# Last RMSNorm and residual of a two-layer encoder on token-major tiles, with the residual input transposed first

## The chip, the cores and the metric

The kernel runs on one core of a Trainium2 chip. The metric is the device time of one execution in microseconds (us). Before the change three runs gave a median of 3404.63 us (3402.58 to 3406.06).

## The reference

The kernel computes a two-layer streaming encoder step, in float32, for 1024 prompt tokens and 8 x 16 tokens of running streams. Only the very last operation matters here: the residual update that ends layer 1.

```
def _rmsnorm(x, g):
    x32 = x.astype(jnp.float32)
    y = x32 * lax.rsqrt(jnp.mean(x32 * x32, axis=-1, keepdims=True) + EPS) * g.astype(jnp.float32)
    return y.astype(x.dtype)

for layer in range(DEPTH):
    ...                                   # mLSTM (layer 0) or differential attention (layer 1)
    x = x + _rmsnorm(h, norm_g[layer, 1])
    h = _swiglu(_rmsnorm(x, norm_g[layer, 2]), ffn_w_in[layer], ffn_w_out[layer])
    x = x + _rmsnorm(h, norm_g[layer, 3])
return x, ...                             # y_prompt (1, 1024, 1024) and y_sample (8, 16, 1024)
```

## The kernel before

Prompt and sample tokens are processed together as 1152 tokens. The stream lies transposed in SBUF: F0 is `[128, 8, 1152]`, with the feature within a block of 128 on the partitions, the 8 blocks (k) next, and the tokens on the free axis. F1 has the same layout and holds what a layer adds, here the output h of the last FFN. The 1152 tokens are cut into 9 tiles of 128 (`tile(i)`) for transposes and stores, and into 3 chunks of 384 (`TC`) for matmuls.

The order of the work is written out by hand, one program for each engine, with semaphores between them. There is no scheduler. PSUM has 8 banks of 512 floats per partition. Matmul outputs of 1152 tokens use two triples of banks in turn, 0 to 2 for even groups and 3 to 5 for odd ones (`G(o)`); `group_free` says that a triple was evacuated. The last group of the last FFN ("ffn1") adds its 8 blocks of output into F1 one by one: TensorE fills a triple (lines 1615, 1619 and 1621 are the three products of a split float32 matmul), VectorE adds it to F1 (L2085), ScalarE squares the finished block (L1818) into one of two buffers SQX, and VectorE adds the squares into ACCX (L2015, L2017).

After the last block ("post3") the kernel before does this:

- TensorE multiplies ACCX and the last square by a matrix of ones (L1711, L1714), so that the sum of squares of each token stands on all 128 partitions.
- ScalarE takes a logarithm (L1824) and an exponential (L1827) of it, each with a load of its function table, which gives 1/rms in RS, `[128, 1152]`.
- VectorE, chunk by chunk (`last_residual`), multiplies the 8 blocks of F1 by gain and RS (L2055) and adds blocks 0 to 3 into F0 (L2059); GpSimd adds blocks 4 to 7 (L1596).
- Chunk by chunk TensorE transposes the finished F0 (`store_y_pe`, L1423, 8 transposes of 128x128 for each tile of 128 tokens, into pairs of banks), ScalarE copies each tile from PSUM into one of three buffers XL (L1432), and SyncE stores it (L1438). XL is used again once its store has landed (`y_sent`).

Of the kernel before, what the change touches and what calls it, by code (L numbers as in the profile page):

```python
# [18 lines left out]
ALU = mybir.AluOpType  # L19
# [3 lines left out]
P = 128  # L23
D = 1024
# [5 lines left out]
NT = T // P  # L30
# [108 lines left out]
def build(nc, x_prompt, x_sample, state_C, state_n, state_m, cache_k, cache_v, norm_g, mlstm_w_in,  # L139
# [4 lines left out]
    with ctx, nc.allow_non_contiguous_dma(reason="a few gates, stabilisers and tables of rows"):  # L144
        def sem(name):
            return ctx.enter_context(nc.semaphore(name))
# [50 lines left out]
        r = Region(XB, XB + 2 * FB)  # L197
        ACCX = r("ACCX", [P, T])
        SQX = [r(f"SQX{i}", [P, T]) for i in range(2)]

        r = Region(*W)
        XL = [r(f"XL{i}", [P, D]) for i in range(3)]
# [182 lines left out]
        def tile(i):  # L385
            return slice(i * P, (i + 1) * P)
# [1021 lines left out]


        y_tr = sem("y_tr")  # L1410
        y_cp = sem("y_cp")
        y_sent = [sem(f"y_sent{i}") for i in range(3)]

        def store_y_pe(pe):
            for i in range(NT):
                if i % 3 == 0:

                    pe.wait_ge(res_ready[0], 3 * KT // 2 + i // 3 + 1)
                    pe.wait_ge(res_ready[1], 3 * KT // 2 + i // 3 + 1)
                if i >= 4:  # L1420
                    pe.wait_ge(y_cp, i - 3)
                for k in range(KT):
                    mm = pe.transpose(PS[:, 2 * (i % 4) + k // 4, (k % 4) * P:(k % 4 + 1) * P], F0[:, k, tile(i)], ident)  # L1423
                mm.then_inc(y_tr, 1)

        def store_y_act(act):
            for i in range(NT):
                act.wait_ge(y_tr, i + 1)
                if i >= 3:
                    act.wait_ge(y_sent[i % 3], 16 * (i // 3))  # L1430
                b = 2 * (i % 4)
                act.activation(XL[i % 3][:, :], PS[:, b:b + 2, :].rearrange("p b c -> p (b c)"), ACT.Copy).then_inc(y_cp, 1)  # L1432
            act.wait_ge(nsv_sent, VSTORED)

        def store_y_sp(sp):
            for i in range(NT):
# [87 lines left out]
        @blocks.gpsimd  # L1524
        def _(pool):
            pool.memset(WRAW[0][:, :, :], 0.0)
            pool.memset(BG[:, :], 0.0).then_inc(s_zero, 1)
            pool.memset(EPSC[:, :], EPS).then_inc(w_split, 2)
            pool.memset(HALF[:, :], -0.5).then_inc(unit_free, 1)
            pool.memset(ZERO[:, 0:1], 0.0).then_inc(group_free[0], 1)  # L1530
            pool.memset(ZERO[:, 1:2], 0.0).then_inc(group_free[1], 1)
            pool.memset(ZERO[:, 2:3], 0.0).then_inc(hf_ready, 1)
            pool.memset(ZERO[:, 3:4], 0.0).then_inc(nsv_sent, 16)
            pool.memset(ZERO[:, 4:5], 0.0).then_inc(nt_cp, 1)

            def split(par, u, landed):
                pool.wait_ge(w_landed[par], landed)
                pool.wait_ge(unit_free, u + 1)

                pool.tensor_tensor(WHI[par][:, :, :], WRAW[par][:, :, :], bc(bc(ZERO[:, 0], KT), P), ALU.add)  # L1540
                pool.drain()
                pool.tensor_tensor(WLO[par][:, :, :], WRAW[par][:, :, :], WHI[par][:, :, :].bitcast(F32),  # L1542
                                   ALU.subtract).then_inc(w_split, 1)

            def pair(first, i):

                for j in range(2):
                    par = (first + j) % 2
                    split(par, first + 2 * i + j, 16 * ((first + j) // 2) + 16 + (0 if par else 16) + 16 * i)

            def single(u):
                split(u % 2, u, 16 * (u // 2) + 16 + (0 if u % 2 else 16))

            def residual(n):

                for k in range(1, KT, 2):
                    pool.wait_ge(res_mul, n * KT // 2 + k // 2 + 1)
                    pool.tensor_tensor(F0[:, k, :], F0[:, k, :], F1[:, k, :], ALU.add).then_inc(res_ready[1], 1)
                pool.drain()

            def run(first, n):
                with pool.Fori(0, n // 2) as i:
                    pair(first, i)

            pool.drain()
            split(0, 0, 32)
            run(U0["q_m"], 24)
            single(U0["out_m"])
            mlstm_pool(pool)
            single(U0["out_m"] + 1)  # L1570
            run(U0["out_m"] + 2, 6)
            single(U0["ffn0"])
            residual(0)
            single(U0["ffn0"] + 1)
            pool.wait_ge(f1_dead, 1)
            pool.memset(F1[:, :, :], 0.0).then_inc(f1_zero, 1)
            run(U0["ffn0"] + 2, 64)
            single(U0["q_a"])
            residual(1)
            single(U0["q_a"] + 1)  # L1580
            run(U0["q_a"] + 2, 22)
            single(U0["out_a"])
            attention_pool(pool)
            single(U0["out_a"] + 1)
            run(U0["out_a"] + 2, 6)
            single(U0["ffn1"])
            residual(2)
            single(U0["ffn1"] + 1)
            pool.wait_ge(f1_dead, 2)
            pool.memset(F1[:, :, :], 0.0).then_inc(f1_zero, 1)  # L1590
            run(U0["ffn1"] + 2, 64)

            for c in range(NC):
                cols = slice(c * TC, (c + 1) * TC)
                pool.wait_ge(res_mul, 3 * KT // 2 + c + 1)
                pool.tensor_tensor(F0[:, 4:8, cols], F0[:, 4:8, cols], F1[:, 4:8, cols], ALU.add).then_inc(res_ready[1], 1)  # L1596


        @blocks.tensor
        def _(pe):  # L1600
# [103 lines left out]
            def norm_sum(name, acc=None, sq=None):  # L1704

                o, n = G0[name], NORMS.index(name)
                free_wait(o, 0, 0)
                if acc is not None:
                    pe.wait_ge(acc_ready, POSTS.index(name) + 1)
                    for c in range(NC):  # L1710
                        pe.matmul(G(o)[:, c, :], ones, acc[:, chunk(c)], start=True, stop=False)  # L1711
                    pe.wait_ge(sq_ready, squares_ready(name, KT - 1))
                    for c in range(NC):
                        mm = pe.matmul(G(o)[:, c, :], ones, sq[:, chunk(c)], start=False, stop=True)  # L1714
                else:
                    for k in range(KT):
                        pe.wait_ge(sq_ready, squares_ready(name, k))
                        for c in range(NC):
                            mm = pe.matmul(G(o)[:, c, :], ones, SQ[k % 2][:, chunk(c)], start=k == 0, stop=k == KT - 1)
                            if k == 0 and c == 0:  # L1720
                                mm.then_inc(unit_free, 1)
                        if k < KT - 1:
                            mm.then_inc(sq_used, 1)
                mm.then_inc(group_ready, 1)
# [78 lines left out]
            norm_sum("post2", ACC, SQ[1])  # L1803
            norm_sum("pre2")
            ffn("ffn1", 6)
            norm_sum("post3", ACCX, SQX[1])
            store_y_pe(pe)


        @blocks.scalar  # L1810
        def _(act):
            def squares(name, src, ready=None, sq=SQ):
                for k in range(KT):
                    if ready is not None:
                        ready(k)
                    if squares_used(name, k - 2) > 0:
                        act.wait_ge(sq_used, squares_used(name, k - 2))
                    act.activation(sq[k % 2][:, :], src[:, k, :], ACT.Square).then_inc(sq_ready, 1)  # L1818

            def root(name):  # L1820

# [176 lines left out]
            root("pre2")  # L1998
            high_norm("ffn1", 4 * KT)
            ffn("ffn1")  # L2000
            squares("post3", F1, lambda k: act.wait_ge(group_free[(G0["post3"] - KT + k) % 2], (G0["post3"] - KT + k) // 2 + 2), SQX)
            root("post3")
            store_y_act(act)


        @blocks.vector
        def _(dve):
# [13 lines left out]
            def rstd(name):  # L2021
                dve.wait_ge(rs_ready, NORMS.index(name) + 1)
# [15 lines left out]
            def residual(gain):  # L2038

                dve.drain()  # L2040
                for k in range(KT):
# [3 lines left out]
                        dve.tensor_tensor(F0[:, k - 1, :], F0[:, k - 1, :], F1[:, k - 1, :], ALU.add).then_inc(res_ready[0], 1)  # L2045
                    else:
                        dve.drain()

            def last_residual(gain):

                dve.drain()
                for c in range(NC):
                    cols = slice(c * TC, (c + 1) * TC)
                    for k in (4, 5, 6, 7, 0, 1, 2, 3):
                        w = dve.scalar_tensor_tensor(F1[:, k, cols], F1[:, k, cols], gain(k), RS[:, cols], ALU.mult, ALU.mult)  # L2055
                        if k == 7:
                            w.then_inc(res_mul, 1)
                    dve.drain()
                    dve.tensor_tensor(F0[:, 0:4, cols], F0[:, 0:4, cols], F1[:, 0:4, cols], ALU.add).then_inc(res_ready[0], 1)  # L2059

            def ffn(name):
                o0, l = G0[name], FFN_L[name]
# [119 lines left out]
            updated(dve, 2, KT - 1)  # L2182
            norm_split(6, lambda k: GN[:, 1, 2, k:k + 1])
            ffn("ffn1")
            rstd("post3")
            last_residual(lambda k: GN[:, 1, 3, k:k + 1])


# [26 lines left out]
```

## Time and profile before

| | |
|---|---|
| median of three runs | 3404.63 us |
| the profiled execution's own time | 3402.93 us |
| its span (first to last instruction of the trace) | 3401.1 us |
| last matmul of the FFN begins to end | about 3351.6 us into the span |
| from there to the end of the span | about 49.5 us |

All figures of the trace are of that one profiled execution. Busy time is not at once time on the critical path: the chain of waits says what the end waited for, and the timeline of one engine says when each instruction began. In the timeline neighbours of the same kind are merged ("x24"), and the time of a merged row runs from the first start to the last end. PE is TensorE, PEld its loads of the stationary operand, DVE VectorE, ACT ScalarE, POOL GpSimd. PEclk is the granted TensorE clock: 1.00 is 2.4 GHz and 0.50 is 1.2 GHz, and a value between them is a stretch with both.

### The profile page before, as it was taken

How to read it: one execution, taken by the hardware profiler on the slowest of the kernel's cores; microseconds unless marked ns; L12 is line 12 of the kernel's file. 1: busy time of each engine (PE TensorE's matmuls, PEld its weight loads, DVE VectorE, ACT ScalarE, POOL GpSimd, SP SyncE). 2: the span in 40 equal slices, each digit the busy share in tenths (PEclk: the TensorE clock that was granted, in tenths of full speed). 3: DMA queues.
4: the chain of work that ended last, by engine and by line, in shares of the span. 5: the costliest groups of instructions: out<-in, count | busy, mean ns of one | idle time of the engine just before them, and what ended most of it. 6: DMA issues, size and time to landing. Idle time of an engine off the chain costs nothing.

```text
span 3401.1 us, 45274 instructions
## 1 busy us (share of the span) xinstructions
PE 3120.9 (92%) x18309; PEld 2947.2 (87%) x18309; DVE 1122.6 (33%) x1561; ACT 727.2 (21%) x1205; POOL 1003.4 (30%) x523
## 2 busy tenths in 40 slices
PE   6999987979999999997889977888979999999996
PEld 6999876959999999996889945566959999999995
DVE  4100254252222222225220058865152222222226
ACT  4111242240000000002222157644140000000002
POOL 2333100433333333333323322110443333333331
PEclk8999877989999999999999989998989999999998
DMA  4121301201111111110212220046201111111111
GB/s 152 43 77 55 94 32 56 93 19 44 44 43 37 43 43 43 40 40 25 87 44 86 88 83 26 13 151 216 94 18 44 44 43 40 40 43 43 43 37 56
DMA packets 237697, 200.90 MB, mean 59 GB/s; under 512 B 8545, under 2 KB 202494, under 8 KB 237074
## 3 DMA queue, kind: packets, MB, share of 16 engines
q1 hardware_dynamic: 194402, 147.93, 14.0%
q10 hardware_dynamic: 43184, 51.46, 4.5%
q8 instruction: 74, 1.21, 0.2%
q14 instruction: 37, 0.30, 0.0%
HBM read 166.30 MB, written 33.06 MB: 59 GB/s over the span
## 4 chain that ended last, share of the span: by engine, by line
PE 80%; DVE 6%; issue 6%; ACT 2%; DVEq 2%; POOL 1%; POOLq 1%; ACTq 1%; DMA 1%; SPq 0%
PE PS L1615 23%; PE PS L1619 23%; PE PS L1621 23%; PE PS L1042 1%; DVE F L2042 1%; PE PS L1088 1%; PE PS L1122 1%; PE PS L1072 1%; PE PS L513 1%; PE PS L1678 1%; PE PS L490 1%; DVE PS L1307 1%; DVE F L2055 1%; DVE XLO L2026 1%; DVEq L1308 1%
## 5 line engine op out<-in xcount | busy, mean ns | idle before, releaser
L1540 POOL TENSOR_TENSOR WHI<-WRAW,ZERO 128x1024 fp32r<-128x1024 f32 x197 | 373.6, 1897 | 1805.6 <-PE PS L1615 1774.3
L1615 PE MATMUL PS<-XHI,WHI 128*128 128x384 f32 x3672 | 848.2, 339 | 63.3 <-DVE XLO L2026 62.9
L1619 PE MATMUL PS<-XLO,WHI 128*128 128x384 f32 x3672 | 839.6, 336 | 0.0
L1621 PE MATMUL PS<-XHI,WLO 128*128 128x384 f32 x3672 | 838.6, 336 | 0.0
L1615 PEld LDWEIGHTS PS<-XHI,WHI 128*128 128x128 f32 x3672 | 656.6, 190 | 74.1 <-issue 55.8
L1619 PEld LDWEIGHTS PS<-XLO,WHI 128*128 128x128 f32 x3672 | 660.7, 189 | 0.0
L1621 PEld LDWEIGHTS PS<-XHI,WLO 128*128 128x128 f32 x3672 | 659.3, 189 | 0.0
L1542 POOL TENSOR_TENSOR WLO<-WRAW,WHI 128x1024 fp32r<-128x1024 f32 x197 | 487.6, 2475 | 28.1
L2085 DVE TENSOR_TENSOR F<-F,PS 128x1152 f32<-128x1152 f32 x176 | 238.3, 1354 | 460.3 <-PE PS L1621 460.3
L2070 DVE TENSOR_TENSOR HF<-PS,SG 128x1152 f32<-128x1152 f32 x44 | 59.7, 1358 | 668.3 <-PE PS L1621 668.3
L1900 ACT ACTIVATE HHI<-HF 128x1152 fp32r<-128x1152 f32 x44 | 51.4, 1168 | 1060.6 <-DVEq L2071 1060.6
L1615 PE MATMUL PS<-HHI,WHI 128*128 128x384 f32 x1056 | 243.5, 338 | 5.3 <-DVE HLO L2073 5.3
L1619 PE MATMUL PS<-HLO,WHI 128*128 128x384 f32 x1056 | 242.8, 338 | 0.0
L1621 PE MATMUL PS<-HHI,WLO 128*128 128x384 f32 x1056 | 242.7, 338 | 0.0
L1615 PEld LDWEIGHTS PS<-HHI,WHI 128*128 128x128 f32 x1056 | 189.6, 188 | 6.6 <-DVE HLO L2073 5.9
L1621 PEld LDWEIGHTS PS<-HHI,WLO 128*128 128x128 f32 x1056 | 190.1, 188 | 0.0
L1619 PEld LDWEIGHTS PS<-HLO,WHI 128*128 128x128 f32 x1056 | 189.9, 188 | 0.0
L2073 DVE TENSOR_TENSOR HLO<-HF,HHI 128x1152 fp32r<-128x1152 f32 x44 | 139.1, 3161 | 56.4 <-ACT HHI L1900 56.4
L1895 ACT ACTIVATE SG<-PS 128x1152 f32<-128x1152 f32 x44 | 50.0, 1136 | 421.3 <-PE PS L1621 421.3
L1307 DVE CUSTOM_DVE_ANT_0 PS<-PS,BROW 128x128 f32<-128x128 f32 (+7 forms) x128 | 97.7, 763 | 21.1 <-issue 17.6
L2032 DVE SCALAR_TENSOR_TENSOR XN<-F,GALL,RS 128x1152 f32<-128x1152 f32 x40 | 58.7, 1467 | 128.3 <-PE PS L1621 86.3
L1042 PE MATMUL PS<-F,F 64*128 64x512 f32 (+3 forms) x384 | 84.1, 545 | 18.2 <-ACTq L1203 14.5
(278 smaller groups left out, 2480.4 us busy)
## 6 DMA issues: line engine op xcount, KB each, us to landing
WRAW<-in_ffn_w_in_dram SPq DMA_DIRECT2D x88, 512.0 KB, 3.7
WRAW<-in_ffn_w_out_dram SPq DMA_DIRECT2D x44, 512.0 KB, 3.6
KC<-in_cache_k_dram SPq DMA_DIRECT2D x16, 1024.0 KB, 9.2
VC<-in_cache_v_dram SPq DMA_DIRECT2D x16, 1024.0 KB, 6.2
WRAW<-in_mlstm_w_in_dram SPq DMA_DIRECT2D x24, 512.0 KB, 3.8
xs_scratch<-F ACTq DMA_DIRECT2D x2, 4608.0 KB, 13.3
F<-xs_scratch ACTq DMA_DIRECT2D x2, 4608.0 KB, 14.4
WRAW<-in_kv_w_dram SPq DMA_DIRECT2D x16, 512.0 KB, 3.8
```

The lines of the kernel that those rows point to most:

```text
L1042: mm = pe.matmul(sflat(n, j, w)[:, c:e], F1[64 * j:64 * j + 64, h, tile(i)], F0[64 * j:64 * j + 64, h, c:e], start=True, stop=True)
L1307: dve.tensor_tensor_reduce(s, s, BROW[n % 2][:, SEQ - w:], -1.0, 3e38, ALU.add, ALU.min, stat(n, 4 + j))
L1540: pool.tensor_tensor(WHI[par][:, :, :], WRAW[par][:, :, :], bc(bc(ZERO[:, 0], KT), P), ALU.add)
L1542: pool.tensor_tensor(WLO[par][:, :, :], WRAW[par][:, :, :], WHI[par][:, :, :].bitcast(F32), ALU.subtract).then_inc(w_split, 1)
L1615: mm = pe.matmul(out[:, c, :], wh, rhs_hi[:, chunk(c)], start=first, stop=False)
L1619: pe.matmul(out[:, c, :], wh, rhs_lo[:, chunk(c)], start=False, stop=False)
L1621: mm = pe.matmul(out[:, c, :], wl, rhs_hi[:, chunk(c)], start=False, stop=last)
L1900: act.activation(HHI[:, t, :].rearrange("p (c t) -> p c t", c=NC), HF[:, :, :], ACT.Copy).then_inc(hh_ready, 1)
L2032: dve.scalar_tensor_tensor(XN[k % 2][:, :], F0[:, k, :], gain(k), RS[:, :], ALU.mult, ALU.mult).then_inc(xn_ready, 1)
L2070: dve.tensor_tensor(HF[:, :, :], G(o), SG[:, :, :], ALU.mult).then_inc(group_free[o % 2], 1)
L2073: dve.tensor_tensor(HLO[:, t, :].rearrange("p (c t) -> p c t", c=NC), HF[:, :, :], HHI[:, t, :].rearrange("p (c t) -> p c t", c=NC).bitcas ...
L2085: dve.tensor_tensor(f, f, G(o), ALU.add).then_inc(group_free[o % 2], 1)
```

## The change

The last norm is applied to token-major tiles, after the transposes. Both operands are now transposed: tile by tile F0 (the residual, kind "x") and F1 (the FFN's output, kind "r"), 18 turns of 8 transposes in place of 9.

- Each turn writes one of three pairs of PSUM banks in rotation: (6, 7), (0, 1), (3, 4). The order is x0, x1, x2, r0, x3, r1, x4, r2, x5, r3, x6, r4, x7, r5, x8, r6, r7, r8. Turn n waits for the evacuation of turn n-3.
- The first three turns of x stand ahead of the sum of squares on TensorE. The sum of squares is formed with ACCX and the last square as the stationary operand and one column of ones moving, so that it comes out as one number for each token and partition (bank 2, 9 columns).
- VectorE turns these 9 columns into mean + eps, GpSimd raises them to the power -0.5 (RT, `[128, 9]`).
- ScalarE multiplies each finished block of F1 by its gain, in place, behind its square. It no longer computes logarithm and exponential.
- x0 to x2 are copied from PSUM into XT by VectorE, x3 to x8 by ScalarE. XT lies where the low half of the split FFN input (XLO) was.
- VectorE joins scaling and residual in one instruction for each tile: XL = r (in PSUM) * RT + XT. `last_residual` and GpSimd's additions are gone.

The core of the diff (waits that only mirror these dependencies are kept where a step uses them):

```
+        XT = at("XT", XB + FB, [P, NT, D])
...
+        Y_E = 3 * (G0["post3"] % 2)
+        Y_L = 3 - Y_E
+        Y_BANKS = (6, Y_E, Y_L)
+        Y_ORDER = [("x", i) for i in range(3)]
+        for i in range(NT):
+            Y_ORDER += [("r", i)] + ([("x", i + 3)] if i + 3 < NT else [])
...
         def store_y_pe(pe):
+            def turn(n):
+                kind, i = Y_ORDER[n]
+                if n >= 3:
+                    prev, m = Y_ORDER[n - 3]
+                    if prev == "r":
+                        pe.wait_ge(y_cp, m + 1)
+                    elif m < 3:
+                        pe.wait_ge(y_xd, m + 1)
+                    else:
+                        pe.wait_ge(y_xa, m - 2)
+                src = F0 if kind == "x" else F1
+                dst = y_pair(kind, i)
+                for k in range(KT):
+                    mm = pe.transpose(dst[:, k * P:(k + 1) * P], src[:, k, tile(i)], ident)
+                mm.then_inc(y_tr, 1)
+
+            turn(0)
+            pe.wait_ge(group_free[G0["post3"] % 2], G0["post3"] // 2 + 1)
+            turn(1)
+            pe.wait_ge(group_free[(G0["post3"] + 1) % 2], (G0["post3"] + 1) // 2 + 1)
+            turn(2)
+            pe.wait_ge(acc_ready, POSTS.index("post3") + 1)
+            pe.wait_ge(sq_ready, squares_ready("post3", KT - 1))
+            for t in range(NT):
+                pe.matmul(PS[:, Y_E + 2, t:t + 1], ACCX[:, tile(t)], ones[:, 0:1], start=True, stop=False)
+                mm = pe.matmul(PS[:, Y_E + 2, t:t + 1], SQX[1][:, tile(t)], ones[:, 0:1], start=False, stop=True)
+            mm.then_inc(y_sum, 1)
+            pe.wait_ge(y_gain, KT)
+            for n in range(3, len(Y_ORDER)):
+                turn(n)
...
+        def store_y_act(act):
+            for i in range(3, NT):
+                act.wait_ge(y_tr, y_turned("x", i))
+                act.activation(XT[:, i, :], y_pair("x", i), ACT.Copy).then_inc(y_xa, 1)
...
+        def store_y_dve(dve):
+            for i in range(3):
+                dve.wait_ge(y_tr, y_turned("x", i))
+                dve.tensor_copy(XT[:, i, :], y_pair("x", i)).then_inc(y_xd, 1)
+            dve.wait_ge(y_sum, 1)
+            dve.tensor_scalar(RT[:, :], PS[:, Y_E + 2, 0:NT], 1.0 / D, EPS, ALU.mult, ALU.add).then_inc(y_mean, 1)
+            dve.wait_ge(y_rstd, 1)
             for i in range(NT):
+                dve.wait_ge(y_tr, y_turned("r", i))
                 if i >= 3:
+                    dve.wait_ge(y_xa, i - 2)
+                    dve.wait_ge(y_sent[i % 3], 16 * (i // 3))
+                else:
+                    dve.drain()
+                dve.scalar_tensor_tensor(XL[i % 3][:, :], y_pair("r", i), RT[:, i:i + 1], XT[:, i, :], ALU.mult, ALU.add
+                                         ).then_inc(y_cp, 1)
+
+        def store_y_pool(pool):
+            pool.wait_ge(y_mean, 1)
+            pool.tensor_tensor(RT[:, :], RT[:, :], bc(HALF[:, 0], NT), ALU.pow).then_inc(y_rstd, 1)
...
                     act.activation(sq[k % 2][:, :], src[:, k, :], ACT.Square).then_inc(sq_ready, 1)
+                    if gain is not None:
+                        act.activation(src[:, k, :], src[:, k, :], ACT.Copy, scale=gain(k)).then_inc(y_gain, 1)
...
-            norm_sum("post3", ACCX, SQX[1])
...
-            root("post3")
...
-            rstd("post3")
-            last_residual(lambda k: GN[:, 1, 3, k:k + 1])
+            store_y_dve(dve)
```

On TensorE, at the end of the program before (CST is the identity or the ones, F0 the stream, waits in brackets):

```order
L1621 MATMUL PS<-HHI,WLO_57 128x384 x3
L1711 MATMUL PS<-ACCX,CST 128x384 [waits acc_ready,group_free0]
L1711 MATMUL PS<-ACCX,CST 128x384 x2
L1714 MATMUL PS<-SQX_75,CST 128x384 [waits sq_ready]
L1714 MATMUL PS<-SQX_75,CST 128x384 x2
L1423 MATMUL PS<-CST,F_49 128x128 [waits res_odd,res_even]
L1423 MATMUL PS<-CST,F_49 128x128 x23
```

The same place in the changed program (F_49 is F0, F_50 is F1; L1450 is the transpose, L1461 and L1462 the sums, which stand nine times):

```order
L1678 MATMUL PS<-HHI,WLO_57 128x384 x3
L1450 MATMUL PS<-CST,F_49 128x128 x24
L1461 MATMUL PS<-CST,ACCX 128x1
L1462 MATMUL PS<-CST,SQX_75 128x1
...
L1450 MATMUL PS<-CST,F_50 128x128 x8
L1450 MATMUL PS<-CST,F_49 128x128 x8
...
L1450 MATMUL PS<-CST,F_50 128x128 x24
```

24 transposes of F0 now stand between the last matmul of the FFN and the sums, and no transpose waits for a residual any more.

On VectorE, from the last addition of squares to the end, before:

```order
L2017 TENSOR_TENSOR ACCX<-ACCX,SQX_74 128x1152 [waits sq_ready]
L2055 SCALAR_TENSOR_TENSOR F_50<-F_50,GALL,RS 128x384 [waits rs_ready]
L2055 SCALAR_TENSOR_TENSOR F_50<-F_50,GALL,RS 128x384 x7
L2059 TENSOR_TENSOR F_49<-F_49,F_50 128x4x384
L2055 SCALAR_TENSOR_TENSOR F_50<-F_50,GALL,RS 128x384 x8
```

and in the changed program (the last row stands for tiles 3 to 8, with the three XL buffers in turn):

```order
L2075 TENSOR_TENSOR ACCX<-ACCX,SQX_74 128x1152 [waits sq_ready]
L1477 COPY XT<-PS 128x1024 [waits y_tr] x3
L1479 TENSOR_SCALAR RT<-PS 128x9 [waits y_sum]
L1488 SCALAR_TENSOR_TENSOR XL_77<-PS,RT,XT 128x1024 [waits y_tr,y_rstd]
L1488 SCALAR_TENSOR_TENSOR XL_78<-PS,RT,XT 128x1024 [waits y_tr]
L1488 SCALAR_TENSOR_TENSOR XL_79<-PS,RT,XT 128x1024 [waits y_tr]
L1488 SCALAR_TENSOR_TENSOR XL_77<-PS,RT,XT 128x1024 [waits y_sent0,y_xa,y_tr]
```

VectorE's 24 multiplications and 3 additions gave way to 3 copies, one small instruction and 9 joined instructions that read PSUM and wait for a turn, for a copy of x and for a store.

## Rows read from the trace of the kernel before

**Rows 1.** The page, chain that ended last: shares of the span by engine.

```profile
PE 80%; DVE 6%; issue 6%; ACT 2%; DVEq 2%; POOL 1%; POOLq 1%; ACTq 1%; DMA 1%; SPq 0%
```

**Rows 2.** Chain in order of time, window 3350 to 3402: start us, us, what.

```profile
3351.05 0.55 PE PS L1621 x3
...
3353.07 1.36 DVE ACCX L2017
...
3354.62 3.85 PE PS L1711 x6
3358.47 1.95 PE PS L1714 x6
...
3360.44 1.22 ACT RS L1824
...
3364.28 0.62 DVE F L2055
...
3390.34 1.77 DVE F L2059
...
3392.15 3.61 PE PS L1423 x16
```

**Rows 3.** Timeline of ScalarE at the end: start us, us, line, shapes, idle before.

```profile
3353.01 1.16 ACT L1818 ACTIVATE SQX<-F 128x1152 f32<-128x1152 f32 x1 [2.01 <-DVE F L2085]
...
3395.79 1.94 ACT L1432 ACTIVATE XL<-PS 128x1024 f32<-128x1024 f32 x2 [0.61 <-PE PS L1423]
```

**Rows 4.** TensorE in stretches of 1 us: busy (instructions), granted clock, DMA share, GB/s.

```profile
3353.00:3354.00 1.00, 0.00 (x0) 1.00 0.00 0
...
3355.00:3356.00 1.00, 1.00 (x2) 0.50 0.00 0
...
3358.00:3359.00 1.00, 1.00 (x5) 1.00 0.00 0
...
3394.00:3395.00 1.00, 1.00 (x7) 0.50 0.00 0
...
3396.00:3397.00 1.00, 0.63 (x6) 1.00 1.02 422
```

**Rows 5.** Timeline of TensorE: transposes at 1.2 and 2.4 GHz, 128-column float32 passes.

```profile
18.80 1.09 PE L1773 MATMUL PS<-CST,XL 128*128 128x128 f32 x8 [1.98 <-DMA XL<-in_x_prompt_dram]
...
2245.03 1.95 PE L1088 MATMUL PS<-VP,PTS 128*128 128x128 f32 x16
...
2271.11 1.97 PE L1122 MATMUL PS<-CST,KC 128*128 128x128 f32 x16
...
3373.65 5.17 PE L1423 MATMUL PS<-CST,F 128*128 128x128 f32 x24 [13.25 <-DVE F L2059]
```

**Rows 6.** Timeline of TensorE in the mLSTM stage: 256-column and 1-column float32 matmuls.

```profile
386.23 0.68 PE L513 MATMUL PS<-CT,F 128*128 128x256 f32 x2
386.75 0.28 PE L514 MATMUL PS<-CTN,F 128*128 128x1 f32 x2
386.89 0.68 PE L490 MATMUL PS<-VN,WT 128*128 128x256 f32 x2
```

**Rows 7.** Groups of VectorE by shape: busy us, mean ns, idle before.

```profile
L2032 DVE SCALAR_TENSOR_TENSOR XN<-F,GALL,RS 128x1152 f32<-128x1152 f32 x40 | 58.7, 1467 | 128.3 <-PE PS L1621 86.3 <-ACT RS L1827 29.4 <-ACTq L1941 9.3
...
L1364 DVE COPY KTS<-PS 128x1024 f32<-128x1024 f32 x16 | 19.6, 1225 | 14.3 <-PE PS L1122 14.1
L790 DVE SCALAR_TENSOR_TENSOR F<-PS,GALL,F 128x128 f32<-128x128 f32 x72 | 19.4, 343 | 0.9
...
L776 DVE SCALAR_TENSOR_TENSOR CT<-CT,WS,PS 128x256 f32<-128x256 f32 x32 | 13.2, 476 | 1.0
...
L755 DVE TENSOR_TENSOR DEN<-PS,DEN 128x4 f32<-128x4 f32 x9 | 1.5, 162 | 0.7
```

**Rows 8.** Groups of GpSimd by shape, the two powers.

```profile
L1002 POOL TENSOR_TENSOR RSTD<-MSQ,HALF 128x8 f32<-128x8 f32 x8 | 13.1, 1639 | 1.2
...
L440 POOL TENSOR_TENSOR DEN<-DEN,HALF 128x4 f32<-128x4 f32 x9 | 9.1, 1009 | 186.9 <-ACT DEN L636 186.9
```

**Rows 9.** DMA issues, window 3370 to 3402: count, KB each, median us to landing.

```profile
out_dram<-XL SPq DMA_DIRECT2D x9, 512.0 KB, 2.6
```

More of the change, by code:

```diff
@@ L1410, in build @@
         y_tr = sem("y_tr")
+        y_gain = sem("y_gain")
+        y_sum = sem("y_sum")
+        y_mean = sem("y_mean")
+        y_rstd = sem("y_rstd")
+        y_xd = sem("y_xd")
+        y_xa = sem("y_xa")
         y_cp = sem("y_cp")
         y_sent = [sem(f"y_sent{i}") for i in range(3)]
-        def store_y_pe(pe):
-            for i in range(NT):
[L1416 to L1424, printed above, removed]
@@ L1426, in store_y_act @@
-        def store_y_act(act):
-            for i in range(NT):
-                act.wait_ge(y_tr, i + 1)
-                if i >= 3:
[L1430 to L1433, printed above, removed]
+        Y_E = 3 * (G0["post3"] % 2)
+        Y_L = 3 - Y_E
+        Y_BANKS = (6, Y_E, Y_L)
+        Y_ORDER = [("x", i) for i in range(3)]
@@ new lines, in build, with y_turned, y_pair @@
+        for i in range(NT):
+            Y_ORDER += [("r", i)] + ([("x", i + 3)] if i + 3 < NT else [])
+        def y_turned(kind, i):
+            return Y_ORDER.index((kind, i)) + 1
+        def y_pair(kind, i):
+            b = Y_BANKS[Y_ORDER.index((kind, i)) % 3]
+            return PS[:, b:b + 2, :].rearrange("p b c -> p (b c)")
+        def store_y_pe(pe):
+            def turn(n):
[27 more added lines that the diff above has]
+                turn(n)
@@ new lines, in store_y_act @@
+        def store_y_act(act):
+            for i in range(3, NT):
+                act.wait_ge(y_tr, y_turned("x", i))
+                act.activation(XT[:, i, :], y_pair("x", i), ACT.Copy).then_inc(y_xa, 1)
+            act.wait_ge(nsv_sent, VSTORED)
+        def store_y_dve(dve):
[5 more added lines that the diff above has]
+            dve.wait_ge(y_rstd, 1)
+            for i in range(NT):
+                dve.wait_ge(y_tr, y_turned("r", i))
+                if i >= 3:
+                    dve.wait_ge(y_xa, i - 2)
[4 more added lines that the diff above has]
+                                         ).then_inc(y_cp, 1)
@@ L1591, in _ @@
             run(U0["ffn1"] + 2, 64)
[L1593 to L1596, printed above, removed]
+            store_y_pool(pool)
         @blocks.tensor
@@ L1811, in _, with squares @@
         def _(act):
-            def squares(name, src, ready=None, sq=SQ):
+            def squares(name, src, ready=None, sq=SQ, gain=None):
                 for k in range(KT):
@@ L2000, in _ @@
             ffn("ffn1")
-            squares("post3", F1, lambda k: act.wait_ge(group_free[(G0["post3"] - KT + k) % 2], (G0["post3"] - KT + k) // 2 + 2), SQX)
-            root("post3")
+            squares("post3", F1, lambda k: act.wait_ge(group_free[(G0["post3"] - KT + k) % 2], (G0["post3"] - KT + k) // 2 + 2), SQX,
+                    lambda k: GN[:, 1, 3, k:k + 1])
             store_y_act(act)
@@ L2047, in residual @@
                         dve.drain()
[L2049 to L2059, printed above, removed]
             def ffn(name):
```

## The prediction

> **What bounds the kernel now.** I read the chain of waits first, over the whole span and then over its last 50 us, after that the timelines of the engines there, and last the groups by shape for the price of each new operation. Over the whole span TensorE holds 80% of the chain [rows 1]. The change does not touch that part: it works behind the last FFN matmul. There the chain is another one [rows 2]. TensorE ends at 3351.6 us, and VectorE's last addition of squares sets the start of the column sums at 3354.62. Sums, logarithm and exponential take until 3364.28, and from there VectorE alone sets the pace: 24 multiplications and 3 additions up to 3392.11. Only then can the last three tiles be transposed. ScalarE's last copy ends at 3395.79 + 1.94 = 3397.73 [rows 3], and store and end take 3401.1 - 3397.73 = 3.37. Of the 46.5 us between 3354.62 and 3401.1 TensorE works 5.8 for the sums [rows 2] and three times about 5 for the transposes. So what is to be gained is at most what lies between a TensorE that never waits and these 46.5 us, and the question is what limits the new tail.
>
> **The change part by part.** All sums are against the profiled execution (3402.93 us with a span of 3401.1); it lies 1.7 us under the median of the runs shown, to which I apply the difference.
>
> *Turns of x0 to x2.* A turn is 8 transposes. At the granted clock of 1.00, 8 take 1.09 us and 16 take 1.97 [rows 5]: 0.88 by the difference, 0.98 by half of the longer row. I take 0.94. At 0.50, 24 take 5.17, so a turn is 1.72. After the FFN, from 3353 to 3354, the clock is still 1.00 [rows 4], so three turns take 2.8 us, from 3351.6 to 3354.4. TensorE waited in this stretch anyway, so they cost nothing. If they came cold, they would end at 3356.8 and cost 2.2. The other wait in front of x2, for the evacuation of the last FFN block, ends when the addition of squares begins (3353.07), before x2 is due.
>
> *Gains on ScalarE.* 8 more instructions of 128x1152, each like the square of 1.16 us. A square came after 2.01 us of idling [rows 3], so a block lasts 3.17 and two such instructions (2.3) fit. The last gain ends at 3353.01 + 1.16 + 1.17 = 3355.3, well before r0 is turned. Cost nothing; without this cover at most the one behind the last square, 1.2.
>
> *Sums.* 18 matmuls with one moving column. A float32 matmul stands as two passes in the trace (three of 384 columns are x6 in [rows 2], one of 1 column is x2 in [rows 6]), so 36 passes, each with its own stationary load. No stretch of only such passes exists. From above: two 256-column and two 1-column passes take 386.89 - 386.23 = 0.66 together, 0.165 each, which gives 5.9 us. From below: a 1-column pair moves the next start by 0.14, 0.07 each, 2.5 us. Nearest is a train of 128-column passes with a new stationary operand each, 16 in 1.95 [rows 5], 0.122 each: 4.4 us. Start 3354.6 as before, end 3359.0. VectorE's three copies of x (1.225 each, [rows 7]) run beside it, 3354.5 to 3358.2.
>
> *1/rms.* VectorE's small instruction 0.16 [rows 7]; the power on GpSimd took 1.009 for 4 columns and 1.639 for 8 [rows 8], 0.157 a column, so 1.80 for 9; below, 1.0 if columns cost nothing, above, 3.3 if it were twice the 8-column row. Three handovers at 0.1 (before, the handover into the sums was 0.19: 3353.07 + 1.36 to 3354.62 in [rows 2]). The result is there at 3361.25. This wait is new and exposed: TensorE has r0, x3 and r1 to turn meanwhile (2.8 us, to 3361.8), but the pair for x4 is that of r0.
>
> *Joined instructions.* Scale and add from PSUM: 343 ns for 128 and 476 for 256 elements [rows 7], 1.04 ns an element, so 1.27 us for 1024. From below 1.22 (a copy), from above 1.47 (the same kind with 1152 elements, from SBUF). r0 is done at 3362.5, and x4 starts at 3362.6.
>
> *The other 12 turns.* 12 x 0.94 = 11.3, TensorE ends at 3373.9. This holds if the ring does not stall: a turn may start when the evacuation three turns back is over, so two turns (1.88) must cover 0.2 + 1.27 + 0.1 = 1.57 of the joined instruction, and 1.02 of a copy fits more easily. Stores: a buffer comes round after three tiles, 5.6 us; joined instruction plus store is 1.27 + 3.37 = 4.6, and a store lands in 2.6 [rows 9]. At 1.47 the ring is still at 1.77.
>
> *End.* r6, r7 and r8 are turned one behind the other, faster than VectorE empties them: r6 is turned at 3372.0, three joined instructions from 3372.2 end at 3376.0. With 3.37 for store and end the span is 3379.4: 21.7 us less. The forecast is 3404.6 - 21.7 = 3383.
>
> **A page against the trace: the clock.** In the last tile group before, only transposes ran; the granted clock was 0.50 at 3394 to 3395 and 1.00 at 3396 to 3397, with TensorE busy throughout since 3392.15 [rows 2, 4]. So a dense train of transposes raised the clock here, and one that is warm should keep it. The Trainium skill, "TensorE: Matmul & The Clock Gate", section "PE-mode transpose", says the opposite: transposes do not count as activity for the clock gate, so it does not open for them. By that rule the tail would run at 1.2 GHz; the rows above contradict it.
>
> **The rivals.** A: cold throughout, as a mechanism of this kernel: the clock falls to 0.50 behind the last FFN matmul and stays there, as it did at 3355 after 3 us without work [rows 4]. x0 to x2 end at 3356.8, 36 sums at 0.215 take 7.7 (to 3364.5), 15 turns at 1.72 take 25.8 (to 3390.3), then 0.3 + 1.27 + 3.37: 3395.2, only 5.9 less than before: 3398.7. For it: every long train of transposes at the end began at 0.50 [rows 5]. Against it: these began after idling, and the clock rose within them. This is also the time by the page's rule.
>
> B: cold for a part. One-column passes leave the array nearly empty, and so may the wait for 1/rms. The clock fell after 3 us without work and was at 1.00 again from 3358 [rows 4], some 3 us later; half of that is lost, 1.5 for one such stretch and 3 for two: 3384.5 to 3386, and 3389 if it happens again among the turns. For it: nothing in the trace shows a stretch of one-column passes that kept the clock.
>
> C: the ring runs in lockstep, each turn beginning only when the one before is evacuated, because the three pairs don't overlap as the code lets them. A turn then costs 1.72 + 0.3 + 1.27 + 0.1 = 3.4 (cold, as TensorE is half idle), 15 of them from 3362.4 (sums cold, 3354.6 + 7.7) end at 3413 with their evacuation, plus 3.4: 3416.8, 15.7 slower, 3420. It decides from (3401.1 - 3.4 - 3359.0) / 15 = 2.6 us a turn. Against it: the code names the evacuation three turns back, and before, three tiles were turned in one train of 5.17 us [rows 5] while ScalarE emptied the first of them.
>
> D: the early turns are not hidden, because x0 to x2 start only with the sums' data: 2.8 later, 3385.8.
>
> **How the numbers follow.** Forecast 0.55, B 0.25, D 0.05, A 0.10, C 0.03, and 0.02 for something smaller between A and no change. The unknown prices move the forecast by -1.9 (sums at 2.5) - 0.8 (power) - 0.2 (joined) and by +1.5 (sums at 5.9) + 1.5 (power) + 0.8 (joined): 3380.1 to 3386.7. B reaches to 3389. With A partly in, and 1 us for the spread of the median, the range is 3379.5 to 3392. About 0.2% (6.8 us) is what a measurement of this kernel can tell from no change: faster needs less than 3397.8. That is all of forecast, B and D, half of the 0.02, and of A the case in which the clock comes back for some turns (0.05): 0.91. Within 0.2%: the rest, 0.06. Slower: C, 0.03.
>
> **What would show each step.** Transposes of F0 directly behind the last FFN matmul, in under 3 us, and the sums starting at about 3354.6. Sums over at about 3359 with the clock at 1.00. The power on GpSimd 1.8 us long, with TensorE idle for under 1 us before x4. After that turns of 0.94 us with VectorE not behind, and joined instructions of 1.27. The granted clock in the turns tells the forecast from A and B, the distance between turns from C, and the start of the first transposes from D. The forecast is wrong if the joined instruction takes much over 1.5, since then VectorE with 9 of them becomes the bound, or if the clock falls for longer than the ring takes.

## The result, and the profile after

The changed kernel takes 3384.82 us (median of 5 runs, 3380.29 to 3388.72) against 3405.11 before (5 runs), a ratio of 0.9941 with a 95% interval of 0.9929 to 0.9952. Timed again with five runs it took 3380.6 against 3402.65, 0.9934 (0.9921 to 0.9948). The forecast was 21.7 us less; the medians differ by 20.3 and 22.1.

A good measure inside a profile is the *tail*: from the end of VectorE's last addition of squares to the end of the span. Before, it ran from 3353.07 + 1.36 = 3354.43 [rows 2] to 3401.1: 46.7 us. After, in the profiled execution (3380.29 us, the fastest of the five; span 3378.5), the chain of waits reads as follows (start us, us, what):

```profile
3352.77 1.36 DVE ACCX L2075
...
3354.23 0.38 PE PS L1461 x2
...
3358.43 13.18 PE PS L1450 x104
...
3371.64 0.37 DVE XL L1488
```

The addition ends at 3354.13, so the tail is 24.4 us, against 25.0 in the forecast. Between this addition and the last tiles TensorE alone is on the chain. Its timeline (start us, us) shows two trains of transposes, where three trains of 24 stood before (one of them is in [rows 5]):

```profile
3351.12 2.78 PE L1450 MATMUL PS<-CST,F 128*128 128x128 f32 x24
...
3358.29 15.05 PE L1450 MATMUL PS<-CST,F 128*128 128x128 f32 x120
```

The first 24 stand where TensorE was idle before; they end at 3353.9, ahead of the sums. The other 15 turns are one unbroken row: the ring of three pairs did not stall by more than 0.1 us here. VectorE, in the place of the multiplications of [rows 2], with GpSimd's power and ScalarE's last gain:

```profile
3354.31 3.49 DVE L1477 COPY XT<-PS 128x1024 f32<-128x1024 f32 x3 [0.18 <-issue]
3358.47 0.17 DVE L1479 TENSOR_SCALAR RT<-PS 128x9 f32<-128x9 f32 x1 [0.67 <-PE PS L1462]
3360.61 1.28 DVE L1488 SCALAR_TENSOR_TENSOR XL<-PS,RT,XT 128x1024 f32<-128x1024 f32 x1 [1.97 <-POOL RT L1493]
...
3371.64 3.67 DVE L1488 SCALAR_TENSOR_TENSOR XL<-PS,RT,XT 128x1024 f32<-128x1024 f32 x3 [0.46 <-PE PS L1450]
```

```profile
3358.72 1.80 POOL L1493 TENSOR_TENSOR RT<-RT,HALF 128x9 f32<-128x9 f32 x1 [32.69 <-DVE RT L1479]
```

```profile
3353.78 1.24 ACT L1876 ACTIVATE F<-F,GALL 128x1152 f32<-128x1152 f32 x1
```

VectorE has 9 instructions of 1.28 us, with gaps before the first seven, where it had 27 without. The granted clock differs from the forecast's picture (stretches of 1 us: busy, instructions, granted clock, DMA share, GB/s; [rows 4] before):

```profile
3357.00:3358.00 1.00, 1.00 (x11) 1.00 0.00 0
3358.00:3359.00 1.00, 1.00 (x8) 0.63 0.00 0
...
3361.00:3362.00 1.00, 1.00 (x8) 0.67 0.00 0
3362.00:3363.00 1.00, 1.00 (x11) 1.00 0.30 106
```

At the end of the one-column sums it fell to 0.50, and 3.4 us later, under transposes alone, it was back. With the first transposes slowed, the wait before x4 that the forecast had put in does not appear.

### The profile page after: what moved, and what is told of

It reads as the page before. It is cut to its first block, busy times and chain, and to the rows that moved or that the text cites. A ratio compares the mean times of both kernels' runs of the same rounds, so it can differ in the third digit from the quotient of the medians.

```text
span 3378.5 us, 45448 instructions
## 1 busy us (share of the span) xinstructions
PE 3122.8 (92%) x18405; PEld 2951.6 (87%) x18405; DVE 1110.3 (33%) x1547; ACT 728.3 (22%) x1206; POOL 996.6 (29%) x521
## 3 DMA queue, kind: packets, MB, share of 16 engines
q8 instruction: 75, 1.23, 0.2%
## 4 chain that ended last, share of the span: by engine, by line
PE 81%; issue 6%; DVE 5%; ACT 2%; DVEq 2%; POOL 1%; POOLq 1%; ACTq 1%; DMA 1%; SPq 0%
PE PS L1672 23%; PE PS L1676 23%; PE PS L1678 23%; PE PS L1044 1%; DVE F L2100 1%; PE PS L1090 1%; PE PS L1124 1%; PE PS L1074 1%; PE PS L515 1%; DVE PS L1309 1%; PE PS L1735 1%; PE PS L492 1%; DVEq L1310 1%; PE PS L1135 0%; PE PS L500 0%
```

## The experiments

Where a run has no timed rounds, its verdict comes from the tail of its profile. The front of the program, which no experiment touched, turned out to end anywhere between 3351.2 and 3363.6 us.

**The changed kernel again.** No edit.

> The changed kernel once more, to see what its spread of 8 us comes from. The tail is counted from the end of VectorE's last addition of squares to the end of the span; it was 46.7 us before the change and 24.4 us in the first profile after it, with one stretch of 3 us at a granted clock of 0.50 behind the sums. Theory (the spread lies in front of the tail): tail 24 to 25 us again, and the addition of squares ends at another time of the span by several us. Rival (the clock in the tail makes the spread): another number of stretches at 0.50 in the tail, each worth about 1.5 us, so a tail of 23 or of 26 to 32 us, and the addition of squares within 1 us of 3354.1.

Measured: 3380.6 us, tail 3353.37 to 3379.3, 25.9 us. The addition of squares ended 0.8 us earlier than in the first profile, and the tail was 1.5 longer. The clock fell already within the sums and stayed down twice as long:

```profile
3356.00:3357.00 1.00, 1.00 (x11) 1.00 0.00 0
3357.00:3358.00 1.00, 1.00 (x7) 0.51 0.00 0
...
3363.00:3364.00 1.00, 1.00 (x7) 0.58 0.76 295
3364.00:3365.00 1.00, 1.00 (x11) 1.00 0.03 4
```

Neither side came out whole. The tail lies outside the theory's 24 to 25 us, and the addition ended within 1 us of 3354.1, as the rival had it. What this run shows is that a longer stretch at 0.50 made the tail 1.5 us longer. Where the rest of the 8 us comes from, two profiles cannot tell; the runs below point to the front.

**Sums with 128 columns moving.**

```
-pe.matmul(PS[:, Y_E + 2, t:t + 1], ACCX[:, tile(t)], ones[:, 0:1], start=True, stop=False)
+pe.matmul(PS[:, Y_E + 2, 8 * t:8 * t + P], ACCX[:, tile(t)], ones, start=True, stop=False)
... (the same for SQX[1]; the mean is read at every eighth column)
```

> The column sums with 128 columns of ones moving in place of one, the same 36 passes. Theory (one-column passes leave the array empty, and therefore the clock falls behind them): granted clock 1.00 from the FFN to the last turn; the sums take 4.0 to 4.4 us as before, turns r0 and x3 take 0.94 in place of 1.7, but x4 then waits for the joined instruction of r0, which ends about 1.3 us after 1/rms, so the tail is only 0.6 us shorter: 23.8. Rival 1 (transposes do not count as work for the clock, so it falls wherever the FFN is over): 0.50 behind the sums as before, tail 24.4. Rival 2 (the clock falls in the wait for 1/rms instead): 0.50 some 3 us later, tail 24 to 25.

Measured: 3381.24 us (ratio 0.9936, 0.9923 to 0.995), tail 3351.16 to 3375.6, 24.4 us. Clock and turns:

```profile
3355.00:3356.00 1.00, 1.00 (x11) 1.00 0.00 0
...
3358.00:3359.00 1.00, 0.16 (x2) 1.00 0.00 0
...
3362.00:3363.00 1.00, 1.00 (x12) 1.00 0.55 213
```

```profile
3355.38 2.78 PE L1450 MATMUL PS<-CST,F 128*128 128x128 f32 x24
3359.07 5.46 PE L1450 MATMUL PS<-CST,F 128*128 128x128 f32 x48 [0.90 <-DVE XL L1488]
3364.99 5.46 PE L1450 MATMUL PS<-CST,F 128*128 128x128 f32 x48 [0.46 <-DVE XL L1488]
```

The sums last as long as with one column (3351.26 to 3355.38, 4.1 us), and the clock stays at 1.00 to the last turn. That speaks for the theory. But the tail is no shorter: what the clock gave, TensorE lost in the wait for 1/rms before x4 (0.90, where the prediction had 0.8) and in a second wait of 0.46 that no theory had named. The 0.6 us were a miss.

**x0 to x2 turned behind the sums.**

```
-            turn(0)
             pe.wait_ge(group_free[G0["post3"] % 2], G0["post3"] // 2 + 1)
-            turn(1)
...
-            turn(2)
...
-            for n in range(3, len(Y_ORDER)):
+            for n in range(len(Y_ORDER)):
... (and VectorE forms mean + eps ahead of its copies of x)
```

> x0 to x2 turned behind the sums in place of ahead of them (and VectorE's mean ahead of its copies of x, so that 1/rms is not held up). Theory (the early turns only fill time in which TensorE waited anyway): TensorE idle for about 3 us behind the FFN, the tail longer by the three turns, 2.8 us, and by what the clock loses: as before the change it falls in the idle time, the sums then run at 0.50 for about 3 us (1.5 more) while the stretch at 0.50 behind the sums is gone or stays: tail 27 to 29. Rival (the early turns were not what counts, since 1/rms is waited for anyway): tail within 1 us of 24.4.

Measured: tail 3363.59 to 3395.3, 31.7 us, 7.3 longer than the first profile's 24.4 and more than either theory said. TensorE (timeline, and clock in stretches of 1 us):

```profile
3363.89 0.35 PE L1458 MATMUL PS<-CST,ACCX 128*128 128x1 f32 x2 [3.15 <-DVEq L2074]
...
3370.39 13.42 PE L1450 MATMUL PS<-CST,F 128*128 128x128 f32 x96
3384.71 5.46 PE L1450 MATMUL PS<-CST,F 128*128 128x128 f32 x48 [0.90 <-DVE XL L1485]
```

```profile
3364.00:3365.00 1.00, 1.00 (x10) 1.00 0.00 0
...
3366.00:3367.00 1.00, 1.00 (x7) 0.50 0.00 0
...
3374.00:3375.00 1.00, 1.00 (x7) 0.50 0.00 0
...
3376.00:3377.00 1.00, 1.00 (x11) 1.00 0.00 0
```

Behind 3.15 us of idling the clock was down from 3365.2 to 3375.4, three times as long as in the first profile of the changed kernel. The sums took 3363.89 to 3370.39, 6.5 in place of 4.1 (2.4 more, counted to the first turn behind them); three turns more stand behind them (2.8); the cold turns behind the sums cost about 1.1 more; and a wait of 0.90 came in, since VectorE waited for a store. Together 7.2. The early turns thus gave about a third of the whole gain: 2.8 us because idle time was filled, some 3.5 because the clock stayed up, and 0.9 because no store was waited for. This rests on one profile.

**The joined instruction in two steps.**

```
-dve.scalar_tensor_tensor(XL[i % 3][:, :], y_pair("r", i), RT[:, i:i + 1], XT[:, i, :], ALU.mult, ALU.add)...
+dve.tensor_scalar(XL[i % 3][:, :], y_pair("r", i), RT[:, i:i + 1], None, ALU.mult)
+dve.drain()
+dve.tensor_tensor(XL[i % 3][:, :], XL[i % 3][:, :], XT[:, i, :], ALU.add).then_inc(y_cp, 1)
```

> The joined instruction of VectorE split in two, scale from PSUM into XL and then add XT. Theory (TensorE bounds the tail only because one VectorE instruction of 1.28 us does a tile): VectorE needs 1.25 + 0.1 + 1.2 = 2.5 us a tile, more than the 1.9 of two turns, so 9 x 2.5 = 22.6 from 1/rms at 3360.6 on, tail 32 us (7.9 longer), TensorE waiting for VectorE at most turns. Rival (TensorE's 15 turns set the pace whatever VectorE does): only the last tiles show, tail 25.7 to 28.

Measured: tail 3353.63 to 3387.1, 33.5 us, 9.1 longer than the first profile of the changed kernel. The clock was down from 3357.2 to 3364.0, as long as in the second profile (25.9 us); against that one the tail is 7.6 longer, near the 7.9 of the theory. Every second turn of TensorE now waits for VectorE:

```profile
3369.11 1.97 PE L1450 MATMUL PS<-CST,F 128*128 128x128 f32 x16 [0.71 <-DVE XL L1490]
3371.60 1.97 PE L1450 MATMUL PS<-CST,F 128*128 128x128 f32 x16 [0.53 <-DVE XL L1490]
3374.10 1.97 PE L1450 MATMUL PS<-CST,F 128*128 128x128 f32 x16 [0.53 <-DVE XL L1490]
```

A period is 2.49 us a tile, VectorE's 1.28 + 1.23 with little between them. TensorE bounds the tail only because one VectorE instruction empties and finishes a tile.

**Six output buffers, with the wide sums.**

```
-        XL = [r(f"XL{i}", [P, D]) for i in range(3)]
+        XL = [r(f"XL{i}", [P, D]) for i in range(6)]
... (a joined instruction waits for a store from tile 6 on only)
```

> The wide sums and six output buffers XL in place of three, so that no joined instruction of tiles 3 to 5 waits for a store. With wide sums alone TensorE waited twice for VectorE in the turns, 0.90 us before x4 (1/rms) and 0.46 before the turn behind r3's joined instruction, whose buffer still held r0; tail 24.4 us. Theory (the second wait is the store of r0, which shares the DMA engines with that of r1): it goes, the first stays, tail 23.9. Rival (the ring of three pairs makes both waits): both stay, tail 24.4.

Measured: tail 3354.73 to 3378.5, 23.8 us. Only the wait for 1/rms is left:

```profile
3358.95 2.78 PE L1450 MATMUL PS<-CST,F 128*128 128x128 f32 x24
3362.64 10.70 PE L1450 MATMUL PS<-CST,F 128*128 128x128 f32 x96 [0.90 <-DVE XL L1489]
```

As the theory said, the second wait was an output buffer that still waited for its store: with wide sums alone the store of r0 landed 4.5 us after it was issued (the median was 2.7), and the joined instruction of r3 began 0.1 us later. The other half of the theory, that this store was late because it shared the DMA engines with that of r1, does not hold. In the first profile of the changed kernel the store of r0 took 4.5 us as well, though the next was issued only 2.3 us behind it and the engines moved almost nothing between 3364 and 3365 (busy, instructions, clock, DMA share, GB/s):

```profile
3363.00:3364.00 1.00, 1.00 (x11) 1.00 0.96 397
3364.00:3365.00 1.00, 1.00 (x12) 1.00 0.07 16
```

There too r3 had to wait for it, if for less: it began 0.1 us behind this landing, and 1.14 us behind the copy of x5 (3365.40), where in the tiles around it the distance is 0.9. Of the 0.67 us in its row, some 0.3 were thus the store's; the copy that the row names is one that r3 does not need. TensorE was hardly held up (0.1 us):

```profile
3366.54 1.28 DVE L1488 SCALAR_TENSOR_TENSOR XL<-PS,RT,XT 128x1024 f32<-128x1024 f32 x1 [0.67 <-ACT XT L1471]
```

What did fall together with the late landing is a packet of instructions, on a DMA queue of its own (queue: packets, MB, share of 16 engines, first profile from 3350 to 3379):

```profile
q8 instruction: 1, 0.02, 0.3%
```

It ran from 3362.9 to 3364.3 there. In all seven profiles whose first store took 4.5 to 4.9 us (the changed kernel twice and the runs up to the next one) such a packet ran while that store was on its way. No run moved it on purpose; see the last version for one in which it came earlier.

**The power done twice, with the wide sums.**

```
+pool.tensor_tensor(RT[:, :], RT[:, :], bc(CST[:, C_ONE], NT), ALU.pow)
+pool.drain()
 pool.tensor_tensor(RT[:, :], RT[:, :], bc(HALF[:, 0], NT), ALU.pow).then_inc(y_rstd, 1)
```

> The wide sums, and GpSimd's power done twice (first to the power 1), 1.8 us more between the mean and 1/rms. Theory (at 2.4 GHz the way to 1/rms sets when x4 can be turned): TensorE's wait before x4 grows from 0.90 to 2.7 us and the tail from 24.4 to 26.2. Rival (the wait is for something else, the copies of x or the ring): tail 24.4 to 24.9.

Measured: tail 3356.24 to 3383.6, 27.4 us, 1.2 more than expected. The wait grew to 2.83 (2.7 expected), which is 1.9 more. The clock fell behind this wait, which no theory had named: 96 transposes took 12.37 us, against 10.70 with six buffers, 1.7 more. The second wait of the wide sums is gone in return:

```profile
3366.07 12.37 PE L1450 MATMUL PS<-CST,F 128*128 128x128 f32 x96 [2.83 <-DVE XL L1488]
```

```profile
3366.00:3367.00 1.00, 0.93 (x8) 0.95 0.11 45
3368.00:3369.00 1.00, 1.00 (x6) 0.50 0.86 344
```

**All of it, and a fourth pair of banks.** Sums with 100 columns moving, those of the last square ahead of the wait for ACCX, six output buffers, r6 turned ahead of x8, and from x4 on four pairs:

```
+        Y_ORDER[14], Y_ORDER[15] = Y_ORDER[15], Y_ORDER[14]
+        Y_PAIRS = (slice(6, 8), slice(0, 2), slice(4, 6), slice(2, 4))
...
+            return PS[:, Y_PAIRS[n % 3 if n < 6 else (n + 1) % 4], :]
```

> Everything that the runs point to: sums with 100 columns moving, those of the last square ahead of the wait for ACCX, six output buffers, from x4 on a ring of four pairs of banks (with banks 2 and 3 once the sums are read), and r6 turned ahead of x8. Theory (the clock, 1/rms and the store were all that held TensorE up behind the FFN): clock 1.00 to the last turn, no wait longer than 0.2 us between the sums and the last transpose, 15 turns in 13.8 us, tail 22.9 us, 1.5 to 3 less than the changed kernel's 24.4 and 25.9. In the time of the whole kernel that is 0.05 to 0.1%, less than the spread. Rival (VectorE or the stores set the end whatever TensorE does): tail 24 to 25.

Measured: 3381.87 us (3380.47 to 3382.74) against 3404.31, a ratio of 0.9928 (0.9915 to 0.9942); tail 3357.73 to 3380.0, 22.3 us. The 15 turns are one row at full clock:

```profile
3361.63 13.57 PE L1454 MATMUL PS<-CST,F 128*128 128x128 f32 x120
```

```profile
3356.00:3361.60 5.60, 5.57 (x50) 1.00 0.00 0
3361.60:3375.20 13.60, 13.51 (x122) 1.00 0.57 235
```

It beats the kernel before; against the changed kernel the intervals overlap, and only the tail, 2.1 us and 3.6 us under the two of the changed kernel, tells them apart. How much each of the five edits gave was not separated. At the end VectorE's last joined instructions stand back to back, so the rest is its and the stores'. Its first three stores were issued 1.3 to 1.4 us apart, no further than those of r0 and r1 with the wide sums, and each landed in 2.6 us; the packet of instructions had come at 3364.0, 1.4 us before the first of them was issued.

**The kernel before again.** No edit.

> The kernel before once more, for a second profile of its tail. Theory (the spread between executions lies in front of the tail, the tail itself is steady): from the end of the last addition of squares to the end 46 to 47.5 us again (46.7 in the first profile), with the addition of squares ending within the 3351 to 3364 us that the changed kernels showed. Rival (the tail before varies with the clock too): a tail that differs by 2 us or more, with another number of stretches at 0.50 under the transposes.

Measured: 3405.46 us, tail 3356.84 to 3403.7, 46.9 us, within 0.2 of the first. TensorE's second train of transposes ran at another clock than in the first profile, and the tail did not change, since VectorE set its pace (this run, the first profile under it):

```profile
3385.34 4.22 PE L1423 MATMUL PS<-CST,F 128*128 128x128 f32 x24 [3.88 <-DVE F L2059]
```

```profile
3382.91 5.38 PE L1423 MATMUL PS<-CST,F 128*128 128x128 f32 x24 [4.08 <-DVE F L2059]
```

In eight profiles after the change the front ended at 3351.2 to 3363.6, and at 3354.4 and 3356.8 before it, so no effect of the change on the front shows. Both ends of this range came from one chip. Within one and the same kernel the two profiles differ by 2.4 us in front and 0.2 in the tail before, and by 0.8 in front and 1.5 in the tail after the change. That most of the spread lies in front is thus likely, but not shown for the changed kernel alone. One place in the front is the mLSTM stage: the window from 380 to 600 us of the run with x late (the latest front), and of the changed kernel under it:

```profile
380.00:600.00 220.00, 180.31 (x933) 0.76 0.20 58
```

```profile
380.00:600.00 220.00, 178.22 (x956) 0.79 0.19 57
```

The 64 matmuls of line 515 took from 381.7 to 509.2 us in the first and from 380.8 to 502.2 in the second, 6 of the 9.5 us between the two fronts. Why the clock was lower in that execution was not tried.

## Why the prediction was right

The direction, the path and the size held: 3383 forecast, 3384.82 and 3380.6 measured. Two of its steps did not, the clock behind the sums and the stores. That the sum came out all the same is in part luck: the clock fell where the forecast kept it at 1.00, and the wait that the forecast had put before x4 was then not needed. The times alone do not tell the forecast from rival B, whose 3384.5 to 3386 holds the first median; the traces do. By the steps, from the end of the last addition of squares:

- *VectorE leaves the path.* Right. Its 27 instructions with 27.8 us on the chain [rows 2] are gone; putting only one instruction more on each tile brought 9.1 us back (7.6 against the profile with the same clock).
- *x0 to x2 are free.* Right: 2.78 us in place of the 2.8 worked out, over before the sums could start. They were worth more than the 2.8, 7.3 us, since without them the clock fell earlier and stayed down longer.
- *Gains on ScalarE are free.* Right: 1.24 us each (1.17 taken), the last over at 3355.0, and the blocks of the FFN still 3.17 apart.
- *Sums.* 4.20 us to the end of the last pass, against 4.4; the nearest row, a train with a new stationary operand for each pass, was the right one. The passes took 0.112 with 1 and with 128 columns.
- *1/rms.* The power 1.80 us, as extrapolated from 4 and 8 columns; joined r0 starts 6.5 us into the tail against 6.8.
- *Joined instruction.* 1.28 against 1.27.
- *The 15 turns.* 15.05 us against 14.9 (2.8, a wait of 0.8, 11.3), but made up differently. The forecast had the clock stay at 1.00 behind the sums; this step failed, and rival B named it: 3.4 us at 0.50 in one profile, 6.8 us in the other. TensorE, slowed by it, no longer had to wait for 1/rms. The two costs overlap, so that B cost nothing in the first profile (24.4 us, as with the wide sums at 1.00) and 1.5 in the second, not 1.5 for each stretch. With the clock kept up the predicted wait came out at 0.90.
- *Stores.* The other step that failed: 1.27 + 3.37 = 4.6 us were to fit into the 5.6 of three tiles. The first store took 4.5 us to land in place of the 2.6 of [rows 9], so that 1.28 + 4.5 = 5.8 did not fit, and at full clock r0 and r1 leave together once 1/rms is there. It cost TensorE 0.46 us with the wide sums and 0.90 with x late, and next to nothing in the changed kernel's profiles (VectorE some 0.3 and TensorE 0.1 in the first). The late landing fell together with a packet of instructions; that this is its cause is argued, not shown.
- *End.* 3378.5 - 3375.31 = 3.19 us behind the last joined instruction against 3.37.

Rival A (cold throughout) is out, as the clock was back at 1.00 from 3362 on, and C (lockstep) too, as the turns of one train follow each other without a gap. By the rule of the Trainium skill ("TensorE: Matmul & The Clock Gate", section "PE-mode transpose") the clock does not open for transposes; the trace disagrees, since it rose under transposes alone between 3361 and 3362, and 120 of them in a row ran at 1.00 in the last version. D is out, as x0 starts at 3351.12, right behind the FFN.

## What to carry to other kernels

At the end of a program, look for work that needs no late result (here the transposes of the residual) and put it ahead of the wait that everything else hangs on; it fills the gap, and here TensorE's clock then stayed up until near the end of the sums. Normalising after the transpose turns a scale per token into a scalar per partition, so that evacuation, scaling and residual become one instruction per tile, and here the tail is bound by TensorE. Once several waits are close to each other, taking one away uncovers the next: here clock, 1/rms and store were mended together, and that gained 2 us where the wide sums alone gained nothing.

## What the runs showed of the hardware that was not expected

- One-column passes did not keep the clock. In three profiles with one-column sums and no long gap ahead of them (twice the changed kernel, two steps) it fell to 0.50 within or right behind them. With x late it fell within them too, but behind 3.15 us of idling, as it did before the change [rows 4]. In the three with 100 or 128 columns and no long wait it stayed at 1.00 through the last turn, and in the fourth, with the power done twice, it stayed at 1.00 until it fell behind a wait of 2.83 us. At 1.00 the passes took the same 0.112 us in both forms.
- A dense train of transposes keeps the clock at 1.00: 13.57 us for 120 of them, 0.113 each, against 0.224 almost wholly at 0.50 (24 in 5.38 us, the first train of the second profile of the kernel before). The prediction's 0.215 is from a train whose last part ran at 1.00 already [rows 5].
- The same instruction, behind a front that no run touched, stood up to 12 us apart from profile to profile, with the clock of the mLSTM stage lower in the latest.
- The first of the nine stores landed late where a packet of 0.02 MB of the instruction queue ran beside it: 4.5 to 4.9 us in seven profiles, against 2.6 in the one after the change in which that packet came before it.
